# VectorE's index mask moved among the attention units, and 64 gathered tokens evicted by ScalarE

## The reference, cut to what matters

```python
h = x @ w_in                                   # 1764 columns, split into a_*, b_*, i_*, c_*
o_a = sliding_window_sink_attn(rope(a_q), rope(a_k), a_v, sinks)     # 8 heads
# b: each query attends to the 64 keys with the best index score
score = sum_over_4_heads(w_idx * relu(q_idx @ k_idx.T)); score = where(causal, score, -inf)
_, idx = top_k(score, 64)                      # topk = min(256, S // 4)
o_b = softmax(mask(q_b @ k_b.T / 8, idx)) @ v_b                      # 4 heads
o_c = mla_attn(...)                                                  # 4 heads, key size 96
x = layer_norm(alpha * x + concat(o_a, o_b, o_c) @ w_out)
# mixture of experts: 16 experts in 4 groups; a token picks a group, then 2 experts in it
h = silu(x @ w_gate[e]) * (x @ w_up[e]); x = layer_norm(alpha * x + sum_e gate[e] * h @ w_down[e])
```

## Time and profile before

| what | before |
|---|---|
| median of 3 runs | 1116.34 us (1115.84 to 1121.16) |
| the profiled execution, its own time | 1116.14 us |
| its span | 1114.3 us |
| PE busy | 1081.2 us, 97% |
| DVE busy | 742.1 us, 67% |
| ACT busy | 543.7 us, 49% |
| POOL busy | 110.6 us, 10% |

### The profile page before, as it was taken

One profiled execution on the slowest core, in us unless ns is written; L12 is line 12 of the kernel. 1 busy time (PEld: TensorE's weight loads), 2 busy tenths in 40 slices (PEclk: granted clock), 3 DMA queues, 4 the chain that ended last, 5 costly groups with the idle time before them and its releaser, 6 DMA issues.

```text
span 1114.3 us, 16890 instructions
## 1 busy us (share of the span) xinstructions
PE 1081.2 (97%) x6604; PEld 915.1 (82%) x6604; DVE 742.1 (67%) x1000; ACT 543.7 (49%) x712; POOL 110.6 (10%) x191
## 2 busy tenths in 40 slices
PE   8999999999999999999999999999999999999996
PEld 8999999999888888889787766777798877667765
DVE  4544635587476666658978835785869868457956
ACT  5344454574454444454753435664346725346741
POOL 3000020100000000025600000000068000000000
PEclk9999999999999999999999999999999999999998
DMA  9763443554465555543311879987354017789971
GB/s 296 225 196 114 136 151 123 162 179 152 151 201 198 191 181 198 190 121 102 136 49 49 298 246 339 370 326 266 104 174 151 2 41 256 270 331 371 358 264 38
DMA packets 122102, 214.70 MB, mean 193 GB/s; under 512 B 8882, under 2 KB 78666, under 8 KB 122032
## 3 DMA queue, kind: packets, MB, share of 16 engines
q1 hardware_dynamic: 119408, 209.38, 54.6%
q0 software_dynamic: 1312, 3.88, 1.1%
q10 hardware_dynamic: 1312, 0.49, 0.2%
HBM read 212.63 MB, written 1.09 MB: 192 GB/s over the span
## 4 chain that ended last, share of the span: by engine, by line
PE 75%; DVE 16%; ACT 4%; DMA 2%; issue 2%; SPq 1%; POOL 0%; ACTq 0%; DVEq 0%
PE ps L963 15%; PE ps L965 15%; PE ps L964 15%; PE ps L1104 7%; DVE wlo L2094 3%; PE ps L1103 3%; PE ps L1068 3%; PE ps L1555 2%; PE ps L999 2%; PE ps L1000 2%; PE ps L1001 2%; PE ps L1034 2%; ACT whi L1690 2%; PE ps L1053 1%; PE ps L1577 1%
## 5 line engine op out<-in xcount | busy, mean ns | idle before, releaser
L2094 DVE TENSOR_TENSOR wlo<-raw,whi 128x2048 fp32r<-128x2048 f32 (+3 forms) x145 | 315.1, 2175 | 186.3 <-ACT whi L1690 185.7
L1690 ACT ACTIVATE whi<-raw 128x2048 fp32r<-128x2048 f32 (+3 forms) x145 | 261.5, 1807 | 163.1 <-PE ps L1104 61.4
L963 PE MATMUL ps<-whi,act_both 128*128 128x256 f32 (+2 forms) x448 | 142.3, 318 | 2.4 <-DVE wlo L2094 1.3
L965 PE MATMUL ps<-whi,act_both 128*128 128x256 f32 (+2 forms) x448 | 140.2, 313 | 0.0
L964 PE MATMUL ps<-wlo,act_both 128*128 128x256 f32 (+2 forms) x448 | 140.2, 313 | 0.0
L1104 PE MATMUL ps<-act_both,whi 128*128 128x512 f32 x344 | 119.1, 396 | 0.6 <-DVE wlo L2094 0.6
L963 PE MATMUL ps<-act_both,whi 128*128 128x256 f32 x408 | 117.4, 288 | 0.0
L965 PE MATMUL ps<-act_both,wlo 128*128 128x256 f32 x408 | 115.4, 283 | 0.0
L964 PE MATMUL ps<-act_both,whi 128*128 128x256 f32 x408 | 115.4, 283 | 0.0
L2094 DVE TENSOR_TENSOR wlo<-arena,whi 128x2048 fp32r<-128x2048 f32 (+1 forms) x36 | 75.9, 2113 | 34.5 <-ACT whi L1690 34.4
L963 PEld LDWEIGHTS ps<-whi,act_both 128*128 128x128 f32 x448 | 85.2, 190 | 11.8 <-issue 3.7
(11 more groups left out here) (332 smaller groups left out, 2057.2 us busy)
## 6 DMA issues: line engine op xcount, KB each, us to landing
raw<-in_w_in SPq DMA_DIRECT2D x45, 1024.0 KB, 5.5
raw<-in_w_down SPq DMA_DIRECT2D x23, 1024.0 KB, 5.0
raw<-in_w_gu SPq DMA_DIRECT2D x22, 1024.0 KB, 5.1
raw<-in_w_out SPq DMA_DIRECT2D x12, 1024.0 KB, 4.9
raw<-in_w_gate SPq DMA_DIRECT2D x24, 512.0 KB, 5.6
raw<-in_w_up SPq DMA_DIRECT2D x24, 512.0 KB, 6.8
arena<-in_w_gate SPq DMA_DIRECT2D x20, 512.0 KB, 5.2
arena<-in_w_up SPq DMA_DIRECT2D x20, 512.0 KB, 6.4
```

The costliest lines, as they stand in the source:

```text
L963: pe.matmul(o, ah, bh, start=first, stop=False)
L965: return pe.matmul(o, al, bh, start=False, stop=last)
L1690: act.activation(whi[:, c % 3, 0:n], raw_of(c, v)[:, 0:n], ACT.Copy).then_inc(hi_made, 1)
L2094: dve.tensor_tensor(wlo[:, c % 3, 0:n], raw_of(c, v)[:, 0:n], whi[:, c % 3, 0:n].bitcast(F32), ALU.subtract)\
```

## The change: what it does

In each of the two layers, the last three of the eight rounds of `strike_out` (5, 6, 7) leave their place before the units: they are made behind the work of the steps 2, 4 and 6 of the unit loop, and the three mask instructions behind the work of step 7. `split(10)`, which stood behind the mask, now follows `split(9)` at once. The number of DVE instructions in this stage stays the same.

At the start of the experts, the eight copies of 64 columns into `xg_pairs` pass from DVE to ACT; each stands ahead of ACT's rounded copy of the same block.

```diff
 (ACT)           def gathered(k):
                     act.wait_ge(xg_full, l * KD + k + 1)
+                    act.activation(xg_pairs[:, k, :], ps[:, k, 2 * P:2 * P + 64], ACT.Copy)
                     act.activation(xg_hi[:, k, 0:2 * P], ps[:, k, 0:2 * P], ACT.Copy).then_inc(xg_h, 1)
 (DVE)           strike_out(4)
                 split(9)
-                strike_out(5)
-                strike_out(6)
-                strike_out(7)
-
-                lk(dve.tensor_scalar(mask_b[:, :], pick[:, :], SEL, 1e30, ALU.is_equal, ALU.mult))
-                for o, w in ((0, S), (S, P)):
-                    lk(dve.scalar_tensor_tensor(out=mask_b[:, o:o + w], in0=mask_b[:, o:o + w], scalar=NEG,
-                                                in1=cst[:, C_MC + S - w:C_MC + S], op0=ALU.add, op1=ALU.add))
+
+                def mask():
+                    (the same three instructions)
                 split(10)
 ...
                         outs(unit_layer(i - 3), nu + (i - 3), lk)
+                    if i in (2, 4, 6):
+                        strike_out(4 + i // 2)
+                    if i == 7:
+                        mask()
 ...
 (DVE)           def gathered(k):
                     dve.wait_ge(xg_h, l * KD + k + 1)
-                    dve.tensor_copy(xg_pairs[:, k, :], ps[:, k, 2 * P:2 * P + 64])
                     dve.tensor_tensor(xg_lo[:, k, 0:2 * P], ...).then_inc(xg_l, 1)
```

More of the change, by code:

```diff
@@ L2452, in layer @@
                 split(9)
-                strike_out(5)
-                strike_out(6)
-                strike_out(7)
-                lk(dve.tensor_scalar(mask_b[:, :], pick[:, :], SEL, 1e30, ALU.is_equal, ALU.mult))
-                for o, w in ((0, S), (S, P)):
-                    lk(dve.scalar_tensor_tensor(out=mask_b[:, o:o + w], in0=mask_b[:, o:o + w], scalar=NEG,
-                                                in1=cst[:, C_MC + S - w:C_MC + S], op0=ALU.add, op1=ALU.add))
+                def mask():
+                    lk(dve.tensor_scalar(mask_b[:, :], pick[:, :], SEL, 1e30, ALU.is_equal, ALU.mult))
+                    for o, w in ((0, S), (S, P)):
+                        lk(dve.scalar_tensor_tensor(out=mask_b[:, o:o + w], in0=mask_b[:, o:o + w], scalar=NEG,
+                                                    in1=cst[:, C_MC + S - w:C_MC + S], op0=ALU.add, op1=ALU.add))
                 split(10)
```

## The result

| | before | after |
|---|---|---|
| median | 1115.44 us (1114.42 to 1121.16, 19 runs) | 1127.33 us (1120.52 to 1140.83, 19 runs) |
| the profiled execution, its own time | 1116.14 us | 1120.52 us |
| its span | 1114.3 us | 1118.7 us |
| PE / DVE / ACT busy | 1081.2 / 742.1 / 543.7 us | 1082.0 / 738.6 / 545.2 us |

The change is slower: the ratio after to before is 1.009, 95% interval 1.0066 to 1.0113. Most of what is to be learned stands in the range of after, 20 us wide. Each execution has a mean granted clock beside its time. Four of the 19, from 1120.52 to 1121.74 us, have 0.998; four, from 1122.06 to 1122.59, have 0.995; the other eleven have 0.973 to 0.993, and by and large the lower it is the longer they are (0.993: 1123.83; 0.986: 1130.37; 0.973: 1140.83).

The account below looks back on a forecast made before the run. The prediction took DVE as leading until unit 5, with PE leading by little behind that. Two layers of +3.9 us less 0.8 for the copies made +7.0 on 1116.14, so 1123.1 us, range 1118.5 to 1126.0.

Parts of the forecast that it names:

- Part 1, the gain in front: Ahead of the units 6.40 us a layer leave DVE; logits 0 start 0.53 us earlier, the rest becomes DVE idle.
- Part 2, up to unit 5: In the units DVE's lateness reaches PE through ACT's exponentials and copies: turn_probs of unit 5 2.2 us late, at 562.4.
- rival 1: In the units PE leads and the rounds fall into slack: 1 to 2 us lost a layer, 1118.3 us; chance 0.19.
- Part 2, the sum of a layer: End of the units: 6.40 us less 0.53 and 2.0 of filled DVE idle, 3.9 us later (3.6 to 4.3).
- mere issue: Units 3 to 5: DVE's unoccupied 0.57 us over 22 instructions, 0.026 each, taken as no room for work.
- GpSimd: Ahead of the units tile 10's earlier split delays rope 4 to about 543.2; PE needs it at 543.77; costed at 0.
- Part 3, the copies: Start of the experts: 64-column copies cost ACT 0.15 us each; moving them gains 0.8 us in all (0.2 to 1.0).
- Rival 4: At the experts the copies on ACT delay the tile behind: 0.8 us more, 1123.9; chance 0.70 together with the forecast.
- Sum, clock at 1.00: Whole kernel: 2 x 3.9 - 0.8 = +7.0 us on the profiled execution's 1116.14, giving 1123.1 us.
- rival 3: In the units DVE's rounds open gaps in PE's work and the clock falls: +6 us a layer, 1135; chance 0.05.

Follow-up runs that it names:

- the fully filled kernel: The changed kernel with idle matmuls of 512 columns where PE waits in steps 3, 5, 7 and 10: median 1120.87 us, ratio 1.0046.

## Why the prediction came near, and where it was wrong

The prediction was 1123.1 us, 1118.5 to 1126.0, slower with 0.66. The change is slower by over 0.5%, as forecast. Its ratio of 1.009 puts it at 1125.5 us (1.009 x 1115.44), inside the range; the median without the three longest executions is 1123.2, that of all 19 is 1127.33, above the range. That 1123.2 meets the forecast is luck: the sum was 2 to 3 us too high, and falls of the clock, which were given 0.05, put as much and more back. The recorded text named a clock under 1.00 in the units as a sign of being wrong, and it came. Point by point:

- **Part 1, the gain in front.** Right. Logits 0 began at 542.73, 0.39 us earlier, not 0.53; the rest is that the columns ended 0.14 later in this execution. 3.61 and 2.21 us of DVE idle took the place of the work, as written.
- **Part 2, up to unit 5.** The chain was right to 0.1 us: logits 5 at 557.83 (557.8), exponentials to 561.4 (561.3), turn_probs of unit 5 at 562.52 (562.4). DVE and not PE leads; rival 1 falls with that.
- **Part 2, the sum of a layer.** The delay is 3.5 us in each layer and not 3.9, 0.1 outside the bounds of 3.6 and 4.3. Of 6.40 us, 0.53 were won before unit 0's logits (counted from the scores) and 2.4 taken up, not 2.0. The timelines say where. At unit 6's logits DVE was 2.63 us behind (560.15 against 557.52); two rounds less the 0.39 make 3.01, so 0.4 had been taken up by then. The third round and the mask add 3.00, and unit 11's logits come 3.59 later (572.88 against 569.29): the units 6 to 11 took 2.0, just as predicted. The mis-sized term is what the units 0 to 5 can take up, put at nothing as "mere issue". The medians of the two kernels without falls of the clock say the same: the changed kernel with step 7 filled less the copies alone with step 3 filled, 1120.51 less 1113.70, is 6.8 us, 3.4 a layer (from two batches, whose kernels before differ by 0.65).
- **GpSimd.** Right. DVE's split at 538.09 now holds rope 4: one of its operations took 2.37 us, the key copies 0.40 and not 2.34. Rope 4 ended at 542.85 and PE, at 543.90, did not wait for it. POOL's timeline:

```profile
538.33 2.37 POOL L895 TENSOR_TENSOR arena<-arena,cst 128x64 f32<-128x64 f32 x1
...
542.40 0.45 POOL L896 TENSOR_TENSOR arena<-arena 128x128 f32<-128x128 f32 x1
542.92 0.40 POOL L941 COPY arena<-arena 128x256 f32<-128x256 f32 x1
```

- **Part 3, the copies.** 1.2 us by the medians and 1.0 by the fastest executions of the copies alone, where I took 0.8 with 1.0 as the upper bound; beside the moved rounds about 2, from two executions. The copy's pitch on ACT is 0.10 and not 0.15. The bound was the sum of PE's waits for `product` in one profiled execution, and it left out the 0.9 us at L1555. Rival 4 did not come.
- **Sum, clock at 1.00.** 2 x 3.5 less 1.2 is +5.8. From the fastest execution of before in this comparison, 1114.42, that makes 1120.2, and the executions of after whose clock stayed up begin at 1120.5. My sum started from a profiled execution 1.7 us above the fastest, so its 1123.1 has two errors of 1.2 and 1.7 us in one direction. A slip beside it: the upper bound of 1126.0 stands for 5.3 us a layer with the copies' 0.8 taken off, not for 4.7.
- **The step that failed is the weighing of rival 3**, the fall of the clock, to which I gave 0.05. Its mechanism and its place, gaps that DVE's rounds open in PE's work, were written down. Against it I held that 545 to 550 had 2.04 us idle at a clock of 1.00, and that new gaps of 1 to 2 us would do no more. That was one execution. Eleven of 19 clearly lost clock, 15 if those at 0.995 are counted, so the median of all is one of them. The price of 6 us a layer lies among those that the traces show for a layer that falls: 1.3, 3.1, 3.2, 7.5 and 9.1 us more in the unit stretch than in an undisturbed layer (1.3 and 7.5 are against the fully filled kernel), and by the estimate above 0.4 and 1.9 in the kernel with the later rounds. The low clock came behind the very gap of the earlier trace rows as well, in the traced execution of the kernel with the mask in step 7, which up to there differs from the kernel before only by the mask's place. The windows of one execution show what can happen, not what happens every time; the range of the three times shown, 1115.84 to 1121.16, could have told me that something of 5 us comes and goes in this kernel.

What stays open is why the gap of step 7 decides and those of 0.90 and 1.02 us beside it do not, why longer waits outside the units do no harm, and why a fall lasts from 3 to 27 us. Up to 560 the execution that fell and the one that didn't agree to 0.1 us. Where the clock fell in the changed kernel's executions at 0.995 is not traced either: it can have been behind the gap of step 3 or of step 7. I also did not trace an execution of the kernel before in which the clock fell; that its long ones come from step 3 is shown only by the filler that takes them away from its near relative.

## What to carry to other kernels

Work of an engine that is moved "into the gaps" must be counted against the idle time of that engine in that stretch: here 6.4 us went into a place with 2.4, and came out of one where PE was the bound and the work was free. Where the engine that is delayed feeds TensorE, look for the new gap between its small matmuls and put a few idle matmuls into it, ahead of the instruction that waits; four of 512 columns in a gap of 1.1 us cost nothing and took away up to 20 us. When a kernel's times scatter by more than 0.3%, list the mean granted clock beside each before taking one profile for the kernel.

## What was not expected of the hardware

- One gap of 1.0 to 1.2 us between small matmuls, in a stretch that has others, was followed in some executions by a granted clock of 0.50 (1.2 GHz) for 3 to 27 us, though PE was busy nearly all that time at the lower clock, and in others by nothing: at least eleven of 19 executions of the changed kernel lost clock, none of 11 with the gap of step 7 filled.
- At 1.2 GHz the same four transposes take 1.09 us instead of 0.63, eight of 64 columns 1.81 instead of 1.00.
- An ACT copy of 64 columns out of PSUM lasts 0.20 to 0.33 us in its own record but delays the next instruction by 0.10.
